# Asking for the experts' down weights from ScalarE's DMA queue instead of SyncE's

## What is computed

```python
# cut from the reference
def expert_block(args):
    tok_b, w_b, e = args                 # up to 128 tokens that chose expert e
    xb = t[tok_b]
    hb = jax.nn.silu(xb @ w_gate[e]) * (xb @ w_up[e])
    return (hb @ w_down[e]) * w_b[:, None]
# w_gate, w_up: (32, 1024, 256); w_down: (32, 256, 1024), per layer
# every token is sent to 2 of 32 experts
y = lax.map(expert_block, ...)
out = jnp.zeros((N, D)).at[buf_tok].add(y)
```

## Time and profile before

| what | value |
|---|---|
| median of 3 runs | 2133.2 us (2132.74 to 2134.62) |
| the profiled execution, its own time | 2132.33 us |
| its span from the first to the last instruction | 2130.5 us |
| first layer's block loop (TensorE) | from 612.4 to 932.2 us of the span |
| second layer's block loop | from 1674.4 to 1983.1 us |
| TensorE's granted clock over the span | 0.973 |

### The profile page before, as it was taken

The page is one execution under the profiler, slowest core; times in us unless marked ns, Lnnn a source line. Parts: engine busy times, 40 slices in busy tenths (PEclk is TensorE's granted clock), DMA queues, the critical chain, the costliest instruction groups (busy, mean ns, idle before and its releaser), DMA issues.

```text
span 2130.5 us, 35243 instructions
## 1 busy us (share of the span) xinstructions
PE 1981.0 (93%) x8952; PEld 1107.7 (52%) x8952; DVE 1028.4 (48%) x2327; ACT 638.6 (30%) x1521; POOL 374.8 (18%) x542
## 2 busy tenths in 40 slices
PE   6999899999879999999979998999998799999898
PEld 3555576655445545544435555776554455445443
DVE  2489778654432111235424897786544321112353
ACT  3333366522111111132133433665221111111311
POOL 2332100021012222210022321000210222221100
PEclk9999999999879999999989999999998899999999
DMA  7011241000499999965210112410013999999522
GB/s 256 15 30 30 67 152 46 11 30 29 169 331 391 382 380 379 390 229 204 85 29 15 30 30 74 145 46 11 30 49 140 356 395 374 374 378 348 179 89 98
DMA packets 122224, 362.00 MB, mean 170 GB/s; under 512 B 18853, under 2 KB 54005, under 8 KB 105220
## 3 DMA queue, kind: packets, MB, share of 16 engines
q1 hardware_dynamic: 105028, 318.74, 41.3%
q0 software_dynamic: 14784, 33.59, 4.3%
q10 hardware_dynamic: 2304, 8.39, 1.0%
HBM read 319.50 MB, written 59.51 MB: 178 GB/s over the span
## 4 chain that ended last, share of the span: by engine, by line
PE 80%; DMA 12%; DVE 3%; issue 2%; ACT 2%; SPq 1%; POOL 0%; ACTq 0%; POOLq 0%; DVEq 0%
PE ps L1845 32%; DMA region_c<-in_moe_w_up_dram 8%; PE ps L2231 7%; PE ps L2019 6%; PE ps L1866 4%; PE ps L2227 4%; PE ps L2252 4%; PE ps L2064 4%; PE ps L2043 3%; PE ps L1814 3%; PE ps L1940 2%; PE ps L2246 2%; PE ps L2153 2%; PE ps L2212 2%; DMA region_a<-in_moe_w_up_dram 2%
## 5 line engine op out<-in xcount | busy, mean ns | idle before, releaser
L1845 PE MATMUL ps<-region_b,region_c 128*128 128x512 f32 x1024 | 449.7, 595 | 3.3 <-DVE region_c L1300 2.8
L1845 PEld LDWEIGHTS ps<-region_b,region_c 128*128 128x128 f32 x1024 | 192.5, 191 | 228.3 <-issue 227.8
L1845 PE MATMUL ps<-region_a,region_c 128*128 128x512 f32 x512 | 224.3, 592 | 0.0
L1725 DVE SCALAR_TENSOR_TENSOR region_a<-region_a,ps 128x128 f32<-128x128 f32 x66 | 23.4, 354 | 385.2 <-ACT region_a L1163 385.2
L2231 PE MATMUL ps<-region_c,region_a 128*128 128x512 f32 x336 | 148.8, 596 | 14.5 <-DMA region_c<-in_moe_w_up_dram 14.5
L2019 PE MATMUL ps<-region_c 96*128 96x512 f32 (+3 forms) x384 | 152.4, 507 | 5.4 <-ACT region_a L1095 4.0
L1845 PEld LDWEIGHTS ps<-region_a,region_c 128*128 128x128 f32 x512 | 96.5, 190 | 116.6 <-issue 116.6
L1163 ACT ACTIVATE region_a<-ps 128x128 f32<-128x128 f32 x66 | 21.8, 330 | 362.8 <-PE ps L2231 243.3
L2231 PEld LDWEIGHTS ps<-region_c,region_a 128*128 128x128 f32 x336 | 62.2, 190 | 94.4 <-issue 94.4
L1501 DVE TENSOR_REDUCE neg_max<-ps 128x1 f32<-128x128 f32 (+7 forms) x128 | 96.8, 756 | 17.5 <-PE ps L2026 14.6
L958 ACT COPY region_c<-ps 128x512 f32<-128x512 f32 x48 | 28.0, 584 | 246.7 <-PE ps L1814 175.7
(11 more groups left out here) (360 smaller groups left out, 3189.1 us busy)
## 6 DMA issues: line engine op xcount, KB each, us to landing
region_c<-in_moe_w_gate_dram SPq DMA_DIRECT2D x44, 1024.0 KB, 10.4
region_c<-in_moe_w_up_dram SPq DMA_DIRECT2D x44, 1024.0 KB, 17.3
region_c<-in_moe_w_down_dram SPq DMA_DIRECT2D x44, 1024.0 KB, 13.0
region_a<-in_moe_w_gate_dram SPq DMA_DIRECT2D x22, 1024.0 KB
region_a<-in_moe_w_up_dram SPq DMA_DIRECT2D x22, 1024.0 KB
region_a<-in_moe_w_down_dram SPq DMA_DIRECT2D x22, 1024.0 KB
region_c<-choice_outputs SPq DMA_DIRECT2D x32, 512.0 KB, 4.5
qk_heads<-gains SPq DMA_DIRECT2D x32, 384.0 KB, 3.9
```

The costliest lines, as they stand in the source:

```text
L1845: ins = mm(dst, lhsT[:, k, :], w[:, k, a:b], start=(k == 0), stop=(k == KD - 1))
```

## The change

In the loop's step, SyncE no longer waits for the down product and no longer asks for the down weights. ScalarE does it, as the last thing of its step: it reads the expert's number of block b+2 from `cells`, waits for `down(b-1)`, and issues the 1 MB load on its own queue. The semaphores that count the landing stay the same. The first three blocks of a layer are still loaded by SyncE alone.

```diff
                     def go():

                         sp.wait_ge(*M_gu.after(prev + b - 1))
-                        e = load_gu(b + 2, last[0])
-                        sp.wait_ge(*M_dn.after(prev + b - 1))
-                        load_dn(e, last[0])
+                        load_gu(b + 2, last[0])
                     guarded(sp, b + 2 < n, go)
...
+                def load_down(b, s, m):
+                    e = act.value_load(cells[0:1, bass.ds(b, 1)], min_val=0, max_val=NE - 1)
+                    act.wait_ge(*M_dn.after(m))
+                    settle(act, passed)
+                    act.dma_start(w_dn[s], I["moe_w_down"][l, e].rearrange("(k p) f -> p k f", p=P)).then_inc(dn_loaded[s], 16)
+
                 def expert(b, here, nxt, last, small, i):
                     m = prev + b
                     guarded(act, b < n, lambda: tanh(m, not small))
                     guarded(act, b + 1 < n, lambda: x_lo(m + 1, small))
                     guarded(act, b <= n, lambda: y_lo(m - 1, small, i))
                     guarded(act, b < n, lambda: h_evac(m, not small))
+                    guarded(act, b + 2 < n, lambda: load_down(b + 2, last[0], m - 1))
```

## The result

The changed kernel takes 2136.3 us (median of 20 runs, 2132.26 to 2138.45), the kernel before in the same comparison 2132.6 us (20 runs). The ratio is 1.0017, 95% interval 1.0010 to 1.0023: 3.7 us or 0.17% slower. The profiled execution spans 2133.0 us (2130.5 before).

A forecast was written before the change was run, and what follows sets the result against it. The loops were taken as bound by TensorE first, then by transfers from about 690 and 1745 us; 2132.3 us plus four terms of 0, plus 0.9 us to the median, gave 2133 us, range 2113 to 2142.

The forecast's parts named there:

- Gate and up earlier: SyncE's gate and up requests in the block loops, 3 to 5 us earlier; taken as 0, bounds 0 and -4.3 us.
- I take 0, since TensorE does not wait there: Where the queue runs dry at the first down products, filling idle engine time was taken to gain 0.
- The bound beside it: Most that earlier requests could gain: 1.9 and 2.4 us of idle engines where the queue runs dry, -4.3 us.
- a request which joins a queue earlier is served no earlier: In the transfer-bound stretches, asking 3 to 5 us earlier behind older requests gains 0.
- Two queues: Gate and up on queue 1, down on queue 10 in the loops; taken as 0, up landing when it did.
- So neither should run away from the other: In the loops, packet turns give bytes 2 to 1, the ratio each block needs, so neither queue gets ahead: 0.
- Down first: Rival: down's queue gets over a third, so up lands last; +5.0 us, once a layer, 2138 us; chance 0.17.
- Mixing costs rate: Rival: each per cent of rate lost in the bound stretches costs 4.4 us, 2% give 2142; chance 0.08 with down starving.
- ScalarE's work: ScalarE's added request and preparation, some 1.5 us per block, fit its 3.24 us idle before tanh; cost 0.
- down asked for 1.5 us later: Down request in each step at 761.3 in place of 759.85 us, covered by 11.7 us of slack; cost 0.
- up landing at 20 to 22 us: In the profile after, up lands 20 to 22 us after its request in place of 17.5.
- waits for up of about 25 us: TensorE waits for up weights in the two loops by about the same 25 us in all as before.

The follow-up runs named there:

- e1: Kernel before, still one queue, but gate and up of block b+2 requested after gate_up(b-1), then down of block b+1 after down(b-2); 2125.6 us, ratio 0.9973.
- e11: Kernel before with e1's early requests only in blocks 1 to 6 of each layer, from block 7 on the old order; 2128.6 us, ratio 0.9980.
- e13: e1 with down requested from ScalarE's queue from block 19 of each layer on; ratio 1.0004 to the kernel before.
- e14: e1 with down requested from ScalarE's queue up to block 18 of each layer, SyncE's after; ratio 0.9986 to the kernel before.
- e3: Kernel before with half blocks' tokens gathered into partitions 64 to 127 in place of 0 to 63; ratio 1.0027.
- e4: Changed kernel with half blocks' tokens gathered into partitions 64 to 127 in place of 0 to 63; ratio 0.9997 to the kernel before.
- e5: Model left out, only 20 blocks' weights streamed per stretch, on one queue or two; one queue 153.1 us, two 153.7 us.
- e15: e1 with all that the change adds to ScalarE's step except the down request itself, which SyncE makes; ratio 0.9971 to the kernel before.
- e10: Model left out, weights streamed on one queue beside nothing, matmuls, copies, gathers, stores, or all; 408 to 413 GB/s beside matmuls, copies, gathers and stores.

## Why the prediction failed, step by step

The forecast was 2133.0 us, no change; measured were 2136.3, inside the range, 0.17% slower. Two of its four zero terms were mis-sized, with opposite signs; that the total came out so near zero is luck, as the two have separate causes.

**Gate and up earlier: taken as 0, measured -5.8 us** (e1; it holds both parts of the early order). The step that failed is "I take 0, since TensorE does not wait there". The bound beside it, -4.3 us for the dry stretches, was the right size: e11, which is early only there, gains 0.20%, 4.3 us (interval 2.1 to 6.2). TensorE does not wait at 626 us, but the bytes not moved there are missing where it leaves the blocks loaded ahead: against e1 the kernel before is level at the second layer's block 8, 2.9 us behind at block 10, and 3.4 at block 30. The other half of the step, that a request which joins a queue earlier is served no earlier, held for the bound stretch as far as e1 and e11 can be told apart (0.07%, within the uncertainty).

**Two queues: taken as 0, measured +9.4 us.** Over the loop the bytes are 2 to 1, as the loads themselves are, but the step "So neither should run away from the other" failed: it took the turns of the earlier trace rows, where both queues had work, for the whole loop. In the trace of e1 all 132 loads of up and down land in the order in which they were asked for; in that of the changed kernel 40 of the 131 neighbours land the other way round. Landing of the down requests between 800 and 862 us, changed kernel and e1:

```profile
DMA to landing us min/median/max: 12.9/14.2/16.4
...
DMA to landing us min/median/max: 20.6/21.9/22.6
```

With requests made within 0.6 us of the same point of the step, down lands 7.7 us sooner through its own queue, where it only waits for its product, and gate and up, which TensorE waits for, a little later (20.7 and 21.8 us in the two loops, 20.3 and 21.0 in e1). TensorE's waits for them are 27.2 us in place of 20.9. Behind the longest of these waits its granted clock was 0.50 (1.2 GHz) for some 3 us. `gate_up` of two full blocks in the second loop of the changed kernel, the first at full clock, the other behind that wait:

```profile
1795.02 7.11 PE L2236 MATMUL ps<-region_a 128*128 128x512 f32 x16 [0.97 <-DMA region_a<-in_moe_w_up_dram]
...
1815.80 8.71 PE L2236 MATMUL ps<-region_c,region_a 128*128 128x512 f32 x16 [2.28 <-DMA region_c<-in_moe_w_up_dram]
```

6.3 us more of waits and 1.6 us of clock are 7.9 of the 8.9 us between the two profiles (2133.0 and 2124.1). This is the way of the rival "Down first"; that it is paid once a layer rests on the traces of e13 and e14. Two things in that rival were off. It was to decide "as soon as down lands ahead of its own block's up"; it cost already while down landed behind up (by 13.9 us at block 5 and 4.3 at block 23 of the changed kernel; 12.3 and 12.3 in e1). And its price of +5.0 us is about half: by the profiles the change ends 1.7 and 7.2 us behind e1 in the two layers.

**What stays open of it.** 7.7 us of landing at a third of 379 GB/s are 1 MB, by an estimate 2.6 us a layer, or 5.1 us of the 9.4. And e11 in one queue holds down 11 to 14 us ahead and is only 0.5 and 1.5 us behind e1. So the lead alone does not account for the whole; the sharing of the engines while it is built was not measured apart. Nor is it known why with the tokens in the high partitions the change gains (e3, e4). And the rival "Mixing costs rate", which e5 refutes for streams alone, is not settled for the loop: the bound stretches move 1.6 and 1.1% less than in e1, which in part is the loss itself seen as a rate, and the hardware queues take 0.8% (first loop) and 1.5% (second) more of the engines' time per MB (84.2% for 56.50 MB, e1 84.5% for 57.14; 83.3% for 69.36, e1 82.8% for 69.98). By the prediction's price that is an estimated 5 us. Against it, the kernel before takes more still (85.9% for 56.80 MB) and is faster than the change.

**Right as forecast:** ScalarE's work at 0 (e15), down asked for 1.5 us later at 0 (no wait of TensorE for down), up landing at 20 to 22 us, waits for up of about 25 us. Two queues add no rate to streams alone (e5). The Trainium skill, page "DMA: Bandwidth & Descriptors", section "Issuing engines are not separate DMA queues", says that issuing from more engines saves only the time of issuing, as all run on the same 16 DMA engines; 411 and 409 GB/s in e5 agree.

## What to carry to other kernels

The loads on one queue landed here in the order asked for, and that order can be set to the order of need. A second queue took it away and brought in first what was not needed first, though the bytes come out in the right ratio. Where a wait stands between two requests, reordering the requests on the same queue (e1: 6 us faster than before, 9 faster than the change) does what the second queue was tried for. Idle DMA time counts even where no engine waits, if a transfer-bound stretch follows (e11: 4.3 us). And a difference of 0.2% can turn round with an edit that seems to have no part in it (e3, e4): before a small gain is carried over, it is to be measured again.

## What the runs showed of the hardware that was not expected

The loop's 375 to 385 GB/s is not an even rate. The changed kernel between 690 and 862 us, in 40 slices of 4.3 us:

```profile
GB/s 413 416 363 383 420 415 356 388 421 422 331 332 407 421 414 274 372 410 414 316 324 415 416 402 317 394 414 417 314 332 374 414 399 232 352 417 422 401 322 383
```

It is the 410 to 420 of the streams, with dips, the lowest slices at 232 to 363, about once every two blocks (19 us). Nothing in e10 makes such dips; their cause is open.

The granted clock of TensorE fell with the long waits of e13. Windows of 10 us around the first, in the columns of the earlier trace rows:

```profile
790.00:800.00 10.00, 5.84 (x37) 3.13 (x37) 1.60 (x4) 1.50 (x4) 2.46 (x4) 0.87 0.87 332
800.00:810.00 10.00, 10.00 (x47) 5.66 (x44) 1.61 (x4) 1.69 (x4) 0.00 (x0) 0.79 0.79 300
810.00:820.00 10.00, 10.00 (x48) 4.93 (x48) 1.94 (x5) 1.53 (x5) 2.40 (x4) 1.00 0.94 341
```

In windows of 2 us the clock is 0.61 from 797 to 799 us, still within the wait of 4.16 us that ends at 798.80, then 0.50 (the lower of the two levels, 1.2 GHz) up to 803, 0.68 up to 805, and 1.00 again. The 32 matmuls behind the wait took 6.36 us in place of 3.67: a wait for a load can cost more than its length. The changed kernel shows the same, smaller, behind its wait of 2.28 us.
